# A hybrid pooling, convolution and attention block: the pointwise product in split form, and the order of work around it

## The reference

```
h = rms_norm(x, ln_g)
u, g_pool, c_a, c_b, g_conv, q, k, v, g_attn = split(h @ w_in)
y_pool = (trailing mean of u over 2/4/8/16 tokens - u) @ pool_w * pool_scale
c = depthwise_conv31(c_a * sigmoid(c_b)) + conv_b
y_conv = silu(layer_norm(c)) @ conv_pw                # 256 x 256, "pointwise"
y_attn = sliding window attention, 8 heads, window 128
y = concat(y_pool*silu(g_pool), y_conv*silu(g_conv), y_attn*silu(g_attn))
out = rms_norm(x + y @ w_out, final_g)
```

## Time and profile before

| | |
|---|---|
| median of 3 runs | 1447.8 us (1447.57 to 1451.19) |
| profiled execution | 1447.65 us, its span 1445.9 us |
| PE, DVE, ACT, POOL busy | 98%, 79%, 35%, 27% of the span |
| granted TensorE clock | 0.999 of full speed |

### The profile page before, as it was taken

How to read it: one execution, slowest core, us unless ns; L and a number is a source line. 1 busy time by engine, 2 the same in 40 slices (tenths; PEclk the granted TensorE clock), 3 DMA queues, 4 the chain that set the end, 5 groups by cost and what they waited for, 6 DMA issues and landing times.

```text
span 1445.9 us, 20083 instructions
## 1 busy us (share of the span) xinstructions
PE 1420.7 (98%) x6992; PEld 1153.0 (80%) x6992; DVE 1136.9 (79%) x2294; ACT 503.0 (35%) x1234; POOL 385.8 (27%) x626
## 2 busy tenths in 40 slices
PE   6999999999999999999999999999999999999997
PEld 5878787887878787878878778787787878888886
DVE  5676757585766757487999988989899978888886
ACT  5544444445445445332112111121121243333332
POOL 4414233322323142130011010010110245555551
PEclk9999999999999999999999999999999999999999
DMA  7226070616142331726033032130327665555531
GB/s 255 124 77 244 26 273 1 254 44 240 51 189 101 113 134 41 278 59 203 1 146 131 16 131 95 65 131 15 145 74 295 258 217 176 168 161 164 161 117 73
DMA packets 78958, 196.82 MB, mean 136 GB/s; under 512 B 14384, under 2 KB 41392, under 8 KB 71216
## 3 DMA queue, kind: packets, MB, share of 16 engines
q1 hardware_dynamic: 64336, 181.40, 33.9%
q10 hardware_dynamic: 14560, 14.68, 3.7%
HBM read 114.27 MB, written 81.79 MB: 136 GB/s over the span
## 4 chain that ended last, share of the span: by engine, by line
PE 95%; DVE 3%; ACT 1%; DMA 1%; issue 0%; SPq 0%; POOL 0%; POOLq 0%; ACTq 0%; DVEq 0%
PE wide L252 14%; PE wide L253 14%; PE wide L254 14%; PE pair L252 12%; PE pair L253 11%; PE pair L254 11%; PE pair L966 3%; PE wide L996 2%; PE wide L997 2%; PE pair L1884 2%; PE turn L953 2%; PE turn L253 2%; PE turn L252 2%; PE turn L254 2%; PE turn L230 1%; DMA a_rows<-in_w_in_dram 1%
## 5 line engine op out<-in xcount | busy, mean ns | idle before, releaser
L1649 DVE SCALAR_TENSOR_TENSOR m_tail<-m_tail,m_taps 128x512 f32<-128x512 f32 x480 | 337.0, 749 | 6.1
L252 PE MATMUL pair<-xT,w_hi 128*128 128x512 f32 x632 | 257.7, 408 | 6.1 <-DVE xT L245 4.4
L253 PE MATMUL pair<-xT,w_lo 128*128 128x512 f32 x632 | 247.5, 392 | 0.0
L254 PE MATMUL pair<-xT,w_hi 128*128 128x512 f32 x632 | 247.1, 391 | 0.0
L107 POOL TENSOR_TENSOR pool_carrier<-pool_carrier 128x1 f32<-128x1 f32 x83 | 25.7, 309 | 618.3 <-DVE m_meanvar L1658 402.7
L1447 POOL TENSOR_TENSOR operand_sums<-m_y 128x512 f32<-128x512 f32 x75 | 101.2, 1350 | 171.8 <-PE wide L254 120.7
L252 PEld LDWEIGHTS pair<-xT,w_hi 128*128 128x128 f32 x632 | 119.2, 189 | 31.1 <-DVE a_q L864 4.8
L254 PEld LDWEIGHTS pair<-xT,w_hi 128*128 128x128 f32 x632 | 118.9, 188 | 25.7
L253 PEld LDWEIGHTS pair<-xT,w_lo 128*128 128x128 f32 x632 | 119.5, 189 | 19.5
L252 PE MATMUL wide<-xT,w_hi 128*128 128x512 f32 x328 | 130.0, 396 | 0.0
L253 PE MATMUL wide<-xT,w_lo 128*128 128x512 f32 x328 | 127.7, 389 | 0.0
(11 more groups left out here) (220 smaller groups left out, 2895.9 us busy)
## 6 DMA issues: line engine op xcount, KB each, us to landing
xT_scratch<-xT SPq DMA_DIRECT2D x16, 2048.0 KB, 15.7
xs<-in_x_dram SPq DMA_DIRECT2D x32, 512.0 KB, 6.4
x_first<-xT_scratch SPq DMA_DIRECT2D x16, 1024.0 KB, 7.5
xT<-xT_scratch SPq DMA_DIRECT2D x16, 1024.0 KB, 9.2
combo_scratch<-stage SPq DMA_DIRECT2D x28, 512.0 KB, 3.2
m_y<-y_scratch ACTq DMA_DIRECT2D x14, 1024.0 KB, 6.6
y_scratch<-y_out SPq DMA_DIRECT2D x8, 1024.0 KB, 5.9
y_scratch<-y_out SPq DMA_DIRECT2D x16, 512.0 KB, 3.0
```

The source lines that it names most:

```text
L252: nc.tensor.matmul(out, w_hi, x_hi, start=first, stop=False)
L253: nc.tensor.matmul(out, w_lo, x_hi, start=False, stop=False)
L254: return nc.tensor.matmul(out, w_hi, x_lo, start=False, stop=last)
L1649: nc.vector.scalar_tensor_tensor(out=conv[:, i, :], in0=h[:, i, j:j + TB], scalar=taps[:, i, j:j + 1], in1=conv[:, i, :], op0=ALU.mult, op ...
```

## The change

- **Pointwise product.** It becomes a `split3` product. ACT copies the SiLU result `hs` into `hs_hi`; DVE subtracts to make `hs_lo` (`split_hs`), behind 18 taps. The weights are split once, on DVE in block 1. `hs_hi` lies over the normalised values `z`, `hs_lo` over `hs`.
- **Order on DVE in a mixer block.** The sums begin at tap 50 instead of 46, and each follows one tap. The pool gating (now `pool_diff` and `pool_gate`) is put between the last taps; the last instruction of a block's list is now a tap.
- **Last mixer block.** Its `pool_gate` moves from output index 5 to indices 12 and 13; its `split_hs` comes at index 1 of output block 1, `pointwise` behind PE's index 2 and `gate_conv` at index 4 there. SyncE's waits for the buffers follow.
- **Attention.** The eight probability transposes stand together, behind the second group of the projection; the last eight stand together ahead of ca0 of the first mixer block.
- **Last row.** The last row that is finished is squared, scaled and stored in two halves of 512; the early half is squared and multiplied with the gain ahead of the last step, and ACT scales it.

```diff
-            return lambda kk: turn_probs(pe, m, j, kk) if kk < KV else None
+            def both(kk):
+                if kk == 1:
+                    for kv in range(KV):
+                        turn_probs(pe, m, j, kv)
+
+            return both
...
+    tail_at = region.at
     tail = sb("tail", [P, 3 * D + 2 * (PAD + TB)])
+    hs_hi = nc.alloc_sbuf_tensor_at("hs_hi", [P, 2, TB], F32R, offset=tail_at + 4 * D)
+    hs_lo = nc.alloc_sbuf_tensor_at("hs_lo", [P, 2, TB], F32R, offset=tail_at + 8 * D)
...
+    pw_lo = nc.alloc_sbuf_tensor_at("pw_lo", [P, 2, CONV_W], F32R, offset=region.at)
     pw = sb("pw", [P, 2, CONV_W])
+    pw_hi = nc.alloc_sbuf_tensor_at("pw_hi", [P, 2, CONV_W], F32R, offset=region.at)
...
+    END_ROWS = SUB * (NB - 1)
+    END_STEPS = 2 * SUB * (NB - 1) + 4
+    END_ROW = 2
+    end_halves = [xs[1][END_ROW][:, half * TB:(half + 1) * TB] for half in range(2)]
+    end_sumsq, end_meansq = sumsq[:, 0, END_ROW:END_ROW + 1], meansq[:, 0, END_ROW:END_ROW + 1]
...
+        def store_end():
+
+            tokens = lambda row: slice((NB - 1) * TB + row * P, (NB - 1) * TB + row * P + P)
+            sp.wait_ge(finished, END_ROWS + 4)
+            sp.dma_start(out[0, tokens(3), :], xs[1][3]).then_inc(stored[1][3], 16)
+            sp.wait_ge(squared, END_ROWS + 6)
+            sp.dma_start(out[0, tokens(END_ROW), TB:], end_halves[1]).then_inc(stored[1][END_ROW], 16)
+            sp.wait_ge(finished, END_ROWS + 5)
+            sp.dma_start(out[0, tokens(END_ROW), :TB], end_halves[0]).then_inc(stored[1][END_ROW], 16)
...
-                    sp.wait_ge(z_turned, 2 * NB)
+                    store_pool(NB - 1)
+                    sp.wait_ge(pw_full, 2 * NB)
                     load_row(1, 1, 2)
-                    sp.wait_ge(pw_full, 2 * NB)
                     load_row(1, 1, 3)
...
+            for i in range(2):
+                act.wait_ge(hs_done, 4 * n + i + 1)
+                nc.scalar.activation(hs_hi[:, i, :], hs[:, i, :], ACT.Copy).then_inc(hs_done, 1)
...
+        def square_end_half(half):
+
+            p = 2 * NB - 1
+            act.wait_ge(added, reads_of(p, STEPS - 1 if half == 0 else 3))
+            act.wait_ge(squared, END_ROWS + (4 if half == 0 else 2))
+            if half:
+                act.wait_ge(out_rstd_step, 2 * SUB * (NB - 1))
+            cell = end_sumsq if half else sumsq[:, 1, END_ROW:END_ROW + 1]
+            nc.scalar.activation(squares[:, 0:TB], end_halves[half], ACT.Square, accum_out=cell).then_inc(squared, 1)
...
+        act.wait_ge(finished, END_ROWS + 3)
+        act.wait_ge(out_rstd_step, END_STEPS + 5)
+        nc.scalar.activation(end_halves[1], end_halves[1], ACT.Copy, scale=rstd[:, 1, END_ROW:END_ROW + 1]).then_inc(squared, 1)
...
+        def split_hs(n):
+            for i in range(2):
+                dve.wait_ge(hs_done, 4 * n + 2 + i + 1)
+                nc.vector.tensor_tensor(hs_lo[:, i, :], hs[:, i, :], hs_hi[:, i, :].bitcast(F32),
+                                        ALU.subtract).then_inc(hs_lo_done, 1)
...
+            if is_block(n, 1):
+                dve.wait_ge(u_mapped, 4)
+                nc.vector.tensor_copy(pw_hi[:], pw[:]).then_inc(constants_ready, 1)
+                dve.wait_ge(constants_ready, 2)
+                nc.vector.tensor_tensor(pw_lo[:], pw[:], pw_hi[:].bitcast(F32), ALU.subtract).then_inc(constants_ready, 1)
+            some_taps(m, r, LEAD, SPLIT_AT)
+            if not first:
+                split_hs(n - 1)
+            some_taps(m, r, SPLIT_AT, GATE_AT)
             if not first:
                 gate_conv(m if r else m - 1, 1 - r)
             some_taps(m, r, GATE_AT, SUMS_AT)
-            window_sums(m, r)
-            if final:
-                some_taps(m, r, SUMS_AT, HELD_TAPS[0])
-            else:
-                some_taps(m, r, SUMS_AT, len(TAP_ORDER))
-                gate_pool(m, r)
-
-        GATE_AT, SUMS_AT = 34, 46
+            for at, (level, i) in enumerate(SUM_STEPS):
+                some_taps(m, r, SUMS_AT + at, SUMS_AT + at + 1)
+                window_sum(m, r, level, i)
+            if not final:
+                some_taps(m, r, HELD_TAPS[0], HELD_TAPS[1])
+                for i in range(2):
+                    pool_diff(m, r, i)
+                    some_taps(m, r, HELD_TAPS[1 + i], HELD_TAPS[2 + i])
+                for i in range(2):
+                    pool_gate(m, r, i)
+                    some_taps(m, r, HELD_TAPS[3 + i], HELD_TAPS[4 + i])
+
+        SPLIT_AT, GATE_AT, SUMS_AT = 18, 34, 50
...
+                if is_last(n, q) and i == 4:
+                    dve.wait_ge(squared, END_ROWS + 3)
+                    nc.vector.tensor_tensor(end_halves[1], end_halves[1], gain[:, TB:], ALU.mult).then_inc(finished, 1)
...
                     elif at == 5:
-                        gate_pool(NB // 2 - 1, 1)
+                        for half in range(2):
+                            pool_diff(NB // 2 - 1, 1, half)
                     elif at == 7:
                         layer_norm_stats(NB - 1)
+                    elif at >= 12:
+                        pool_gate(NB // 2 - 1, 1, at - 12)
                     if q == 1 and HELD <= i < HELD + 2:
                         finish(0, 0, 0, i - HELD)
                 elif i < 2:
                     if is_block(n, 1) and at == 1:
-                        gate_conv(NB // 2 - 1, 1)
+                        split_hs(NB - 1)
                     if q:
                         finish(n, b, 0, i)
                     else:
                         finish(n - 1, 1 - b, 1, i)
+                elif is_block(n, 1) and at == 4:
+                    gate_conv(NB // 2 - 1, 1)
...
+        dve.wait_ge(out_rstd_step, END_STEPS + 5)
+        nc.vector.scalar_tensor_tensor(out=end_halves[0], in0=end_halves[0], scalar=rstd[:, 1, END_ROW:END_ROW + 1],
+                                       in1=gain[:, 0:TB], op0=ALU.mult, op1=ALU.mult).then_inc(finished, 1)
...
-            pe.wait_ge(hs_done, 2 * n + 2)
+            if is_block(n, 0):
+                pe.wait_ge(constants_ready, 3)
+            pe.wait_ge(hs_lo_done, 2 * n + 2)
             for o in range(2):
+                cols = slice(o * P, (o + 1) * P)
                 for i in range(2):
-                    last = nc.tensor.matmul(feat[o][:], pw[:, i, o * P:(o + 1) * P], hs[:, i, :],
-                                            start=(i == 0), stop=(i == 1))
+                    last = split3(nc, feat[o][:], pw_hi[:, i, cols], pw_lo[:, i, cols], hs_hi[:, i, :], hs_lo[:, i, :],
+                                  i == 0, i == 1)
...
-                attention.turn_last(pe, 0)
-                project(m, r, "ca0", lambda kk: attention.turn_last(pe, 1) if kk == 2 else None)
+                for kv in range(2):
+                    attention.turn_last(pe, kv)
+                project(m, r, "ca0")
...
-                    elif at == 13:
-                        pointwise(NB - 1)
+                elif is_block(n, 1) and at == 2:
+                    pointwise(NB - 1)
```

More of the change, by code:

```diff
@@ L1406, in sync @@
             for row in range(SUB):
-                sp.wait_ge(stored[b][row], 16 * (NB // 2))
+                sp.wait_ge(stored[b][row], 16 * (NB // 2) + (16 if (b, row) == (1, END_ROW) else 0))
         sp.wait_ge(y_pool_stored, 16 * NB)
@@ L1693, in gate_pool, with window_sum @@
[L1693 to L1707 removed]
+        def window_sum(m, r, level, i):
+            n, width = 2 * m + r, 2 ** level
+            cur = sums[:, i, (level - 1) % 2, :] if level else u[:, i, :]
+            dst = sums[:, i, level % 2, :]
+            if level == 0:
+                dve.wait_ge(proj_free[bank_of(r, f"u{i}")], earlier(m, r, f"u{i}") + 1)
+            elif level == 1:
+                dve.wait_ge(sum_step, 4 * n + i + 1)
+            else:
+                dve.wait_ge(sum_step, 4 * n + level + 1)
+            add = nc.vector.tensor_tensor(dst[:, 2 * width:], cur[:, 2 * width:], cur[:, width:HALO + TB - width],
+                                          ALU.add)
+            add.then_inc(sums_done if level == 2 * i + 1 else sum_step, 1)
@@ L1838, in vector @@
         out_blocks(dve, out_body)
-        for order in range(2):
-            finish(NB - 1, 1, 1, order)
+        dve.wait_ge(out_rstd_step, END_STEPS + 3)
+        nc.vector.scalar_tensor_tensor(out=xs[1][3], in0=xs[1][3], scalar=rstd[:, 1, 3:4], in1=gain[:], op0=ALU.mult,
+                                       op1=ALU.mult).then_inc(finished, 1)
+        dve.wait_ge(out_rstd_step, END_STEPS + 5)
+        nc.vector.scalar_tensor_tensor(out=end_halves[0], in0=end_halves[0], scalar=rstd[:, 1, END_ROW:END_ROW + 1],
+                                       in1=gain[:, 0:TB], op0=ALU.mult, op1=ALU.mult).then_inc(finished, 1)
     def tensor(pe):
```

86 lines of the change are left out of this document (47 added, 39 removed).

## The result

The changed kernel takes 1451.93 us (median of 20 executions, 1448.07 to 1452.75), the kernel before 1448.86 us (median of 20, 1447.16 to 1452.22). The ratio is 1.0018 with a 95% interval of 1.0011 to 1.0025: some 2.6 us (1.6 to 3.6) slower, where 2.3 us faster was forecast. The profiled execution took 1451.85 us; its span is 1450.1 us, 4.2 more than before.

The account below looks back on a forecast made before the run. TensorE, busy 98% of the span, was taken to bound the kernel. The terms -5.0 (pointwise product), +1.8 (block 1), +2.1 (output start), -0.3 (transposes) and -0.9 (end) gave -2.3 us: 1445.5 us, range 1441.5 to 1448.0.

Parts of the forecast that it names:

- the last product's wait: Output block 1, ahead of the last pointwise product: TensorE waits for `hs_lo`, done 1.6 us after it is wanted.
- the first section: From the start of the program to `turn_conv` in block 1: forecast -0.3 us.
- the section to output block 0: Up to `turn_conv` in output block 0, with a product and the wait at index 4: forecast +2.1 us.
- the end: After the last matmul: square, `finish` and transfer in halves, forecast -0.9 us (-0.4 to -1.3).
- The waits at index 11 (0.5) and `turn_z` (0.3): Output stage: TensorE was to wait 0.5 us at index 11 and 0.3 us at `turn_z`.
- the wait in block 2: Ahead of `turn_conv` in block 2: TensorE waits for block 1's last tap, +1.8 us (1.4 to 2.4).
- the price of a tap that follows its own kind: DVE in mixer blocks: a tap depending on the one just ahead takes 0.79 us, otherwise 0.667.
- the third rival: Regrouping gives DVE nothing: +1.4 us in block 1, +0.8 at the output start, 1447.7 us; chance 0.04.
- the rule named there: Trainium skill's page: each DVE instruction waits for the one ahead to drain, so regrouping taps would give nothing.
- the row loads: Output start: x rows issued at 1129.5, landing near 1134.0, so TensorE waits 2.6 us at index 4.
- Rival 2: Output start: rows land later than 1134.0, no gain from 2.3 us more, 1449.6 at twice the landing time; chance 0.06.
- The joined transposes: Attention: joining the transposes saves a matmul's slower start behind a group, -0.3 us (0 to -1).

Follow-up runs that it names:

- e1: The changed kernel with 25 extra matmuls, results thrown away, that keep TensorE busy in its two long output-stage waits; 1448.53 us, 1.0001 of the kernel before.
- e4: The changed kernel with three more copies of the pointwise weights on DVE in block 1, lengthening TensorE's wait in block 2; 1454.07 us, ratio 1.0040 to before.
- e8: The changed kernel, but GpSimd waits for the last product's `split_hs` before its operand sum at index 1 of output block 1; 1448.03 us, one run.
- e3: The changed kernel with the last product's `split_hs` moved to the end of DVE's list for output block 0; 1445.86 us, ratio 0.9984 to before.
- e5: The changed kernel with both edits: last mixer block's sums together behind tap 46, last `split_hs` at the end of output block 0's list; 1440.88 us, ratio 0.9946.
- e7: As e5, but all mixer blocks have the old DVE order of sums, taps and pool gating; 1440.49 us, ratio 0.9947 to before.
- e6: As e5, but in mixer block 1 the pool gating stands behind the last tap again; 1439.46 us, ratio 0.9938 to before.
- e2: The changed kernel, but in the last mixer block the sums stand together behind tap 46, the remaining taps behind them; 1445.94 us, ratio 0.9985 to before.

## Why the prediction was wrong

**The step that failed** is the sentence "The stretches with TensorE at work have the clock at full speed (1.00, the 2.4 GHz level), so no clock term is in the sum." It read the clock of a kernel whose longest wait, at full clock, was 1.81 us and kept it for one in which it had itself put waits of 2.6 and 1.6 us. They came as 2.92 and 3.17, and the half clock behind them cost 1.6 and 2.9 us: 4.5 of the 6.5 us between forecast and trace. e1 shows that it hangs on TensorE standing still, e4 that it needs no busy chip. Without this term the profiled execution would be some 0.3 us under the one before, and not 2.3. The other 2 us are the last product's wait (1.6 more, against 0.8 for two small waits that did not come), the first section, with the start of the program in it (0.6), the section to output block 0 (0.4) and the end (0.35).

**The second** is the size of the last product's wait, 3.2 instead of 1.6. `split_hs` was priced at 1.2, the subtraction's distance in the earlier trace rows, at a place where GpSimd adds. There it took 2.35, and the operand part ahead of it 1.09. e8 gave both back. This second error also carries most of the first: behind the 1.6 us that were forecast no half clock was due, for e8's wait of 1.68 had none. The trace of the kernel before had the price already, a subtraction of the same form with GpSimd's addition beside it:

```profile
1164.30 1.34 DVE L1745 TENSOR_TENSOR x_first<-m_y,x_first 128x512 fp32r<-128x512 f32 x1
```

The rest of that chain was right. The waits at index 11 (0.5) and `turn_z` (0.3) did not come in the kernel after, since TensorE had lost more ahead of them; the one at index 11 is in e1 to e3 and e5 to e7, with 0.34 or 0.35 us.

**Right, and with right sizes:** the product at 2.72 us (-0.72 in each block); the wait in block 2, 1.61 recorded and 1.75 by the block's length (1.8 forecast); the price of a tap that follows its own kind, by e6 and e7, so that the third rival and the rule named there fall; the row loads (issue, landing and the wait at index 4 within 0.3 us or so). Each of these needed the order of the instructions and one duration from a row. Rival 2 named this place, but for a later landing; the rows landed when forecast. The kernel is slower for another reason.

**The joined transposes** gave somewhat more than -0.3. The same projection matmul in the third and in the eighth attention block, before, and then after (PE timelines):

```profile
172.44 0.50 PE L252 MATMUL pair<-xT,w_hi 128*128 128x512 f32 x1 [0.31 <-DVE xT L245]
...
567.83 0.50 PE L252 MATMUL pair<-xT,w_hi 128*128 128x512 f32 x1 [0.31 <-DVE xT L245]
```

```profile
173.29 0.50 PE L252 MATMUL pair<-xT,w_hi 128*128 128x512 f32 x1 [0.31 <-DVE xT L245]
...
568.27 0.50 PE L252 MATMUL pair<-xT,w_hi 128*128 128x512 f32 x1 [0.31 <-DVE xT L245]
```

That is 395.39 and 394.98 us for five blocks: 0.08 a block, 0.65 in eight. The first section grew by 0.3 all the same, since the start of the program took longer (see the end). **The end** gave 0.55 of 0.9: ACT's square takes 0.43 and DVE's scaling 0.53 less, as forecast, but POOL's first step, which now adds two parts, takes 0.45 instead of some 0.19, and the last transfer ends 3.4 us behind the scaling, where it was 3.3.

What stays open is when such a wait brings the half clock. The wait of 3.15 to 3.17 us ahead of the last product had it in after and e4 and not in e2, the one of 2.75 to 2.92 at index 4 in all four profiles that have it unfilled (after, e3, e4, e8); no profile here has a wait between 1.81 and 2.75 us at full clock.

## What to carry to other kernels

A wait of the bounding engine is not over when it ends: where TensorE would stand still for some 3 us, put the clock's price (here 1.4 to 2.9 us) into the sum as a case of its own, and look at the distance between matmul starts behind each wait, not at the busy share. Before an instruction is moved to the end of a list, follow its semaphore through every queue to the transfer that it releases; here one order for all blocks was harmless in blocks 2 to 6, cost 1.8 us in block 1 and 4.6 us in the last, and undoing it there, with `split_hs` seven instructions earlier and one block's gating back, turned 0.18% slower into 0.62% faster (0.48% to 0.76%). Price a DVE instruction with two SBUF inputs by rows of the place it goes to, with GpSimd at work or not.

## What the runs showed of the hardware

- Waits of TensorE of 1.61 to 1.81 us never had the half clock behind them (before, after, e1 to e3, e5, e8); waits of 2.75 to 3.17 us had it seven times out of eight in the profiles. By the starts it ended 3.1 (e3) to 6.1 us (after, e4) behind the end of the wait.
- At the very start of the program the matmuls also run at 0.43 us a start at first, in some runs longer than in others: the last such start is at 18.7 us in e3 and at 20.8 us in e8. From the first projection matmul to 643 us or so these two, with the same code there, took 627.4 and 629.0 us. How much of the spread between executions of one kernel (1447.2 to 1452.2 us before) this is, no profile shows.
- A DVE subtraction of 128x512 with both inputs in SBUF took 0.68 or 0.69 us in the mixer blocks of the kernel after (14 of `split_hs`). In its output stage the 42 without a GpSimd addition beside them took as long, and the 65 with one took 0.68 to 1.75, the longer the more of the addition fell into the same time. In e2 two convolution taps beside such an addition took 1.66 and 1.58 us instead of 0.75.
